# Hybrid S5 and sparse-attention step: chunk scan moved beside the bisection, index scores moved forward

## The reference, cut to what matters

```
h = RMSNorm(x);  [u|q|k|v|q_idx|k_idx|w_idx|g_ssm|g_attn] = h @ W_in
A: state space model: 32 groups x 16 channels, 64 complex states each,
   h_t = a*h_(t-1) + b*u_t (associative scan over positions), y = Re(C h_t) + D u_t,
   y = gelu(y); y = y * sigmoid(y @ w_glu)
B: I[t,s] = sum_h w[t,h] * relu(q_idx[t,h] . k_idx[s]);  top 256 of each causal row;
   softmax attention with QK-RMSNorm and T5 bias over the selected keys
x = x + W_o(sigmoid(g_ssm)*(A @ w_ssm_out) + sigmoid(g_attn)*(B @ w_attn_out))
x = x + W_down relu(W_up RMSNorm(x))^2
```

## Time and profile before

| what | value |
|---|---|
| median of 3 runs | 2018.72 us |
| profiled execution, device time | 2016.42 us |
| its span | 2014.6 us |
| PE busy / DVE busy | 1776.4 (88%) / 998.6 (50%) us |
| ACT busy / POOL busy | 562.2 (28%) / 398.6 (20%) us |
| mean granted PE clock | 0.952 |

### The profile page before, as it was taken

One profiled execution on the slowest core, in us unless ns is written; L12 is line 12 of the kernel. 1 busy time (PEld: TensorE's weight loads), 2 busy tenths in 40 slices (PEclk: granted clock), 3 DMA queues, 4 the chain that ended last, 5 costly groups with the idle time before them and its releaser, 6 DMA issues. The chain is left out here.

```text
span 2014.6 us, 28381 instructions
## 1 busy us (share of the span) xinstructions
PE 1776.4 (88%) x11098; PEld 1572.4 (78%) x11112; DVE 998.6 (50%) x1953; ACT 562.2 (28%) x1069; POOL 398.6 (20%) x213
## 2 busy tenths in 40 slices
PE   2869566999999988885598995999999999999999
PEld 2849335899999955553398995988999999999987
DVE  3845988999995547652143132233333333333334
ACT  4323250222322245441121033222222222222220
POOL 5217100011120000000043134111122111111110
PEclk9979788999999989998699997999999999999999
DMA  5171008353231111006542311111111111111102
GB/s 141 47 119 49 27 16 74 98 161 109 93 99 43 39 50 43 1 1 199 167 152 74 117 56 42 42 42 42 42 42 42 44 56 46 42 42 42 42 21 86
DMA packets 120469, 135.34 MB, mean 67 GB/s; under 512 B 23490, under 2 KB 101282, under 8 KB 120338
## 3 DMA queue, kind: packets, MB, share of 16 engines
q1 hardware_dynamic: 120370, 134.01, 23.5%
HBM read 109.80 MB, written 24.18 MB: 67 GB/s over the span
## 5 line engine op out<-in xcount | busy, mean ns | idle before, releaser
L2510 DVE TENSOR_TENSOR view_at<-psum,view_at 128x512 f32<-128x512 f32 (+1 forms) x288 | 199.3, 692 | 183.0 <-PE psum L141 183.0
L139 PE MATMUL psum<-mix_hi,up_hi 128*128 128x352 f32 x768 | 249.9, 325 | 15.9 <-DVE hid_lo L2501 12.3
L140 PE MATMUL psum<-mix_lo,up_hi 128*128 128x352 f32 x768 | 248.1, 323 | 0.0
L141 PE MATMUL psum<-mix_hi,up_lo 128*128 128x352 f32 x768 | 247.8, 323 | 0.0
L139 PE MATMUL psum<-dn_hi,hid_hi 128*128 128x512 f32 x576 | 227.8, 395 | 0.0
L141 PE MATMUL psum<-dn_hi,hid_lo 128*128 128x512 f32 x576 | 226.8, 394 | 0.0
L140 PE MATMUL psum<-dn_lo,hid_hi 128*128 128x512 f32 x576 | 226.4, 393 | 0.0
L2501 DVE TENSOR_TENSOR hid_lo<-psum,hid_hi 128x352 fp32r<-128x352 f32 x96 | 50.4, 525 | 353.8 <-ACT hid_hi L2467 353.8
L1423 DVE TENSOR_SCALAR_CACHE_REDUCE view_at<-view_at,view_at 128x384 bf16<-128x384 f32 (+6 forms) x231 | 196.0, 912 | 1.2
L139 PE MATMUL psum<-h_hi,w_hi 128*128 128x352 f32 x600 | 195.1, 325 | 0.2 <-issue 0.2
L141 PE MATMUL psum<-h_hi,w_lo 128*128 128x352 f32 x600 | 193.5, 323 | 0.0
(11 more groups left out here) (351 smaller groups left out, 3448.8 us busy)
## 6 DMA issues: line engine op xcount, KB each, us to landing
view_at<-w_in SPq DMA_DIRECT2D x18, 1024.0 KB, 5.4
view_at<-w_up SPq DMA_DIRECT2D x16, 1024.0 KB, 5.6
view_at<-w_down SPq DMA_DIRECT2D x16, 1024.0 KB, 4.9
gate_dram<-view_at SPq DMA_DIRECT2D x48, 176.0 KB, 1.9
view_at<-gate_dram SPq DMA_DIRECT2D x16, 528.0 KB, 4.5
view_at<-cache_k SPq DMA_DIRECT2D x32, 256.0 KB, 3.7
view_at<-cache_v SPq DMA_DIRECT2D x32, 256.0 KB
view_at<-u_dram SPq DMA_DIRECT2D x16, 290.0 KB, 14.9
```

Of the source, the lines that this page charges most:

```text
L139: nc.tensor.matmul(out, lhs[0], rhs[0], start=start, stop=False)
L140: nc.tensor.matmul(out, lhs[0], rhs[1], start=False, stop=False)
L141: return nc.tensor.matmul(out, lhs[1], rhs[0], start=False, stop=stop)
L2510: nc.vector.tensor_tensor(x1[r, i, cols], psum[r, 4 + (2 * par + j) % 4, :], x1[r, i, cols], ALU.add).then_inc(add_done, 1)
```

## The change

In stage 1 the 13 parameter loads other than g1 go from SP's to GpSimd's DMA queue, behind GpSimd's first four instructions; g1 is loaded by SP behind the second x tile and has a semaphore of its own; the first gain waits for it alone. The bias copies get four buffers. The loads of `Uc` leave the stage.

In stage 2 the sets, the start states, `turn` and the scan are gone. The 48 units follow the projections at once, with three pairs of banks instead of four, and 9 value units (chunk 5) stand between them, one after every second pair from unit 5 to unit 37. Page loads go ahead of the load of chunk 5. SP loads `Uc` after the last unit.

In stage 3 PE makes sets and start states, 9 value units, the gates, and only then the output of branch A. ACT copies all sets. POOL builds `turn` and does both rotations of each part; DVE keeps only the real scans, as 8 scans over 128 elements a part, ahead of steps 9, 10, 13 and 16 of the bisection. The loads of the kernel table and of u stand behind the 36th gate. The gelu goes from the gates to behind the 19th q and k unit; state output and bias loads are behind the gates.

```diff
+                sp.dma_start(g1c[:, :], a["norm1_g"].rearrange("l (k p) -> p (l k)", p=P)).then_inc(g1_in, 16)
+            for i in range(2, 4):
+                load_x(i)
...
-                sp.dma_start(bias_dram[h], diag[:, h % 2, :]).then_inc(bias_st[h % 2], 16)
+                sp.dma_start(bias_dram[h], diag[:, h % 4, :]).then_inc(bias_st[h % 4], 16)
...
+            pool.dma_start(par_in[0:GP, 0, :], a["ssm_a_re"].rearrange("l (g h) p -> (l g) (h p)", h=2)).then_inc(par_loaded, 16)
...
+            for r, name in enumerate(("ssm_b_re", "ssm_b_im")):
+                pool.dma_start(Bin[:, r], a[name].rearrange("l (g h) p i -> (l h p) g i", h=2)).then_inc(par_loaded, 16)
+            for r, name in enumerate(("ssm_c_re", "ssm_c_im")):
+                pool.dma_start(cin[:, r], a[name].rearrange("l (m g) o p -> (l g o) m p", g=8)).then_inc(par_loaded, 16)
...
-                    dve.wait_ge(par_loaded, 16 * 14)
+                    dve.wait_ge(g1_in, 16)
                 if i:
                     gain(i - 1)
             gain(NT - 1)
+            dve.wait_ge(par_loaded, 16 * 13)
...
+    FILL = [5 + 4 * n for n in range(NT)]
...
+            for n in range(NT):
+                sp.wait_ge(v_out, n + 1)
+                sp.dma_start(rows(nv, n)[:, 0:WC], vst1[own(n), n % 2, :]).then_inc(v_st[n % 2], 16)
+            load_w(sp, 7)
+            sp.wait_ge(unit_mm, len(UNITS))
+            sp.wait_ge(qiS_done, 2)
+            for t in range(L):
+                sp.dma_start(Uc[GI * t:GI * (t + 1), :, :],
+                             u_dram.rearrange("(g i) t c -> t i g c", i=GI)[L - 1 - t]).then_inc(uc_in, 16)
...
-            act.wait_ge(dve_scanned, 1)
...
-                if u == 12:
+                if u == 20:
                     split_high(act, 6)
+                if u in FILL:
+                    n = FILL.index(u)
+                    act.wait_ge(v_mm, n + 1)
+                    if n >= 2:
+                        act.wait_ge(v_st[n % 2], 16 * (n // 2))
...
-                if u >= 4:
-                    pe.wait_ge(relu_done, u - 2)
+                if u >= 2:
+                    pe.wait_ge(relu_done, u - 1)
...
+                if u + 1 in FILL:
+                    n = FILL.index(u + 1)
+                    if n == 0:
+                        pe.wait_ge(w_lo_done, 6)
+                    if n >= 2:
+                        pe.wait_ge(v_out, n - 1)
+                    for k in range(KD):
+                        last = split_mm(psum[:, 6 + n % 2, 0:WC], h_parts(k, tok0(n), tok0(n) + P), w_parts(5, k, 0, WC),
+                                        k == 0, k == KD - 1)
+                    last.then_inc(v_mm, 1)
...
+    SCAN_AT = {9: 0, 10: 1, 13: 2, 16: 3}
...
+                if n == 35:
+                    sp.wait_ge(m_zero, 1)
+                    for t in range(L):
+                        b = L - 1 - t
+                        sp.dma_start(M[GI * b:GI * (b + 1), :, GI * t:P],
+                                     kern_dram[:, :, 0:P - GI * t]).then_inc(m_in, 16)
+                    for t in range(L):
+                        sp.dma_start(Uy[GI * t:GI * (t + 1), :, :],
+                                     u_dram.rearrange("(g i) t c -> t i g c", i=GI)[L - 1 - t][:, :, 0:YC]).then_inc(uy_in, 16)
...
+            link(pool.memset(S[:, :, :, 0:1], 0.0))
+            pool.wait_ge(out_done, I0 + 1)
...
+            for r, (x, y, op) in enumerate(((start[0], start[1], ALU.subtract), (start[1], start[0], ALU.add))):
+                link(tt(t1, a4[0], x, ALU.mult))
+                link(tt(t2, a4[1], y, ALU.mult))
+                link(tt(t1, t1, t2, op))
+                link(tt(ends[:, r].rearrange("p b g -> p g b"), t1, late[r], ALU.add))
...
+            for k in range(7):
+                if k == 6:
+                    split_low(pool, 7)
...
+            def into_frame(q):
+                sr, si, cr, ci, ta, tb, tc, td = parts(q)
+                link(tt(ta, cr, sr, ALU.mult))
+                link(tt(tb, ci, si, ALU.mult))
+                link(tt(tc, cr, si, ALU.mult))
+                link(tt(td, ci, sr, ALU.mult))
+                link(tt(ta, ta, tb, ALU.add))
+                ins = tt(tc, tc, td, ALU.subtract)
+                link(ins)
+                pool.memset(mark, 0.0).then_inc(rotated, 1)
...
+            def out_of_frame(q):
+                sr, si, cr, ci, ta, tb, tc, td = parts(q)
+                pool.wait_ge(summed, q + 1)
+                link(tt(ta, cr, tb, ALU.mult))
+                link(tt(tc, ci, td, ALU.mult))
+                link(tt(sr, ta, tc, ALU.subtract))
+                link(tt(ta, cr, td, ALU.mult))
+                link(tt(tc, ci, tb, ALU.mult))
+                link(tt(si, ta, tc, ALU.add))
...
+            split_low(pool, 8)
+            into_frame(0)
+            into_frame(1)
+            split_low(pool, 9)
+            out_of_frame(0)
+            into_frame(2)
+            split_low(pool, 10)
+            out_of_frame(1)
+            into_frame(3)
+            split_low(pool, 11)
+            out_of_frame(2)
+            out_of_frame(3)
+            link(pool.tensor_copy(finp, S[:, :, :, NC]))
+            pool.memset(mark, 0.0).then_inc(scanned, 1)
             pool.memset(M, 0.0).then_inc(m_zero, 1)
...
+                if n == 2 * NT:
+                    for mm_ in range(4):
+                        act.wait_ge(yt_in[mm_], 16)
+                        nc.scalar.activation(y2[:, mm_, 0:SEQ].rearrange("p (c t) -> p t c", t=L), Yt[:, mm_, :, 0:NC],
+                                             ACT.Gelu_apprx_tanh).then_inc(gelu_done, 1)
+                        nc.scalar.activation(y2[:, mm_, SEQ:T].rearrange("p (b t) -> p t b", t=NS), Yt[:, mm_, 0:NS, NC + 1:YC],
+                                             ACT.Gelu_apprx_tanh).then_inc(gelu_done, 1)
...
+            def sums(q):
+                dve.wait_ge(rotated, q + 1)
+                ta, tb, tc, td = rot[q % 2]
+                for to, of in ((tb, ta), (td, tc)):
+                    for g in range(4):
+                        along = r8[:, 4 * q + g:4 * q + g + 1].broadcast_to([P, NC])
+                        ins = v.tensor_tensor_scan(to[:, g, :], along, of[:, g, :], 0.0, ALU.mult, ALU.add)
+                ins.then_inc(summed, 1)
             for bit in range(31, -1, -1):
+                if 31 - bit in SCAN_AT:
```

More of the change, by code:

```diff
@@ L698, in hybrid_kernel @@
     HR = H * NS
[L699 to L704, removed]
-    qiT = view(36568, 4, T)
[L706 to L712, removed]
+    qiT = view(36568, 4, T)
+    pg = view(31896, NB, NPG, HD)
+    Rb = view(31896, NG, LS)
+    vst1 = view(33944, 2, WC)
+    kiT = view(34456, T)
+    kw = view(35512, NT, HD + H)
+    kwT = view(50600, T)
+    R = view(50600, 2, SEQ)
+    kbT = view(50600, BG, LS)
     wsc = small(NT, H)
@@ L862, in _ @@
-            t1, t2 = (end_t[:, r] for r in range(2))
-            for r, (x, y, op) in enumerate(((start[0], start[1], ALU.subtract), (start[1], start[0], ALU.add))):
-                link(tt(t1, a4[0], x, ALU.mult))
-                link(tt(t2, a4[1], y, ALU.mult))
-                link(tt(t1, t1, t2, op))
-                link(tt(ends[:, r].rearrange("p b g -> p g b"), t1, late[r], ALU.add))
+            split_low(pool, 4)
             split_low(pool, 5)
-            pool.wait_ge(dve_scanned, 1)
@@ L956, in _ @@
             link(v.memset(wsel, 0.0))
-            dve.wait_ge(turned, 1)
-            for q in range(2):
-                scan(v, link, q)
             dve.wait_ge(kw_ev, 2)
@@ L964, in _ @@
             dve.wait_ge(wsc_done, 1)
-            for q in range(2, 4):
-                scan(v, link, q)
-            v.memset(nmark, 0.0).then_inc(dve_scanned, 1)
             for u, (i, h) in enumerate(UNITS):
@@ L1252, in _, with link @@
         def _(pool):
+            tt = nc.gpsimd.tensor_tensor
+            chain = [0]
+            def link(ins):
+                chain[0] += 1
+                ins.then_inc(pool_chain, 1)
+                pool.wait_ge(pool_chain, chain[0])
+            link(pool.memset(S[:, :, :, 0:1], 0.0))
+            pool.wait_ge(out_done, I0 + 1)
+            start = [S[:, r, :, NC + 1:NC + 1 + NB] for r in range(2)]
+            late = [S[:, r, :, NC + 2 + NB:SC] for r in range(2)]
+            a4 = [aps4[:, r, :].unsqueeze(2).broadcast_to([P, GP, NB]) for r in range(2)]
@@ new lines, in _ @@
+            for k in range(7):
+                if k == 6:
+                    split_low(pool, 7)
+                lo = 1 << k
+                n = lo - 1
+                link(pool.tensor_copy(turn[:, :, :, lo], phase[:, :, k, :]))
+                if not n:
+                    continue
+                er, ei = (phase[:, r, k, :].unsqueeze(2).broadcast_to([P, GP, n]) for r in range(2))
+                fr, fi = (turn[:, r, :, 1:lo] for r in range(2))
+                t1, t2 = (x[:, 0:GP * n].rearrange("p (g c) -> p g c", c=n) for x in turn_t)
+                link(tt(t1, fr, er, ALU.mult))
```

(12 more changed lines are left out.)

362 lines of the change are left out of this document (141 added, 221 removed).

## The result

The changed kernel takes 2034.0 us in the median of 4 runs (2033.0 to 2036.2), the kernel before 2019.3 beside it: ratio 1.0074, 95% interval 1.0057 to 1.0092. It is slower by 15. The forecast's sum was 2034, the value stated 2032, the range 2006 to 2058. The profiled execution has a span of 2031.7 against 2014.6, so 17.1 are to be placed. Among the experiments, the first run of e4 (2617.1 and 2016.0) was profiled in a slow execution, at a clock of 0.64, and its trace is not used.

A forecast was written before the change was run, and what follows sets the result against it. Joins bound stage 1, DVE most of stage 2's score units and the third stretch, PE q and k. Terms -15 - 9 + 32 + 7 = +15 gave 2031, with 2.3 for the median 2034; stated 2032, range 2006 to 2058.

The forecast's parts named there:

- Two of the signs: Signs of a right forecast: stage 2 starting at 134 to 138; PE idle some 50 before its first q and k transposes.
- Front and end of stage 1: Stage 1: 2 won by the earlier first gain, 13 by the earlier end; 15 together.
- The cycle of two pairs and one value unit: Stage 2's score units: P + 2.85 + P + R, P a pair on PE, R one relu; 74 for the stretch.
- 9 + 1 - 1: Stage 2's sum: 9 won, bounds 3 and 18.
- Third stretch: Stretch to the masks, DVE: 14 for scans, 8 for short operations and 10 for scans meeting GpSimd; 32 longer.
- The upper end of 52: Third stretch: upper bound on the 32, if GpSimd wins each race for the ports, 36 where 8 was taken.
- no part in it: Third stretch: PE, with 250 of work and a wait of about 10, is done some 50 before DVE's 314.
- q and k: q and k stretch: the gelu, 11 in ACT's chain, stops PE, 7 lost, bounds 3 and 11; nothing else changes.
- the meetings are no small thing: Against the rival that bisection hardly notices GpSimd: third stretch costs 14 instead of 32, time 2016; chance 0.28.
- GpSimd didn't win every race: Against the rival that GpSimd wins every race in the third stretch: +20 over the forecast, 2054; chance 0.17.
- its DMA queue was quick: Against the rival that GpSimd's queue is slow: the front of stage 1 loses 13 instead of winning 2, 2049; chance 0.12.
- value units did interleave: Against the rival that value units do not interleave in stage 2: 27 more there, 2061; chance 0.04.

The follow-up runs named there:

- e4: The kernel after without DVE's 32 scans, GpSimd's table and rotations as they are: 2012.0 us (0.9972).
- e6: The kernel before with all of the change's stage 1, GpSimd issuing the eight loads of u behind the last bias store: 2015.6 us (0.9990).
- e2: The kernel after with the nine value units of chunk 5 back in the third stretch: 2016.3 us (0.9994).
- e7: The kernel after with value units back in the third stretch, four pairs of banks for the score units, and gelu ahead of q and k: 2000.7 us (0.9920).
- e3: The kernel after without GpSimd's rotation table and its 48 rotations, DVE's scans kept: 2001.3 us (0.9930).
- e1: The kernel after with the loads of branch A's output and the gelu moved ahead of the first q and k unit: 2025.5 us (1.0046).

## Why the prediction was right

The mechanism was right in its main parts, and the sizes nearly. That the sum and the time agree to the microsecond, 2034 and 2034, is luck. For the profiled execution the terms summed to 2031, and it took 2033.5 (its span and the 1.8 around it); the 2.3 that I carried to the median were there 0.5, and the two misses cancel. Each term was within 3, with errors of -3, +2, +1, +1 and +2 in the order of the table. Two of the signs that I had named did not come: stage 2 started at 131.35, not at 134 to 138, and PE was idle 31, not 50.

*Front and end of stage 1.* The front was worth 5.6 (u's projection at 54.0 instead of 59.6), not 2: I had spread the cost of a load on GpSimd's queue over 0 to 2, and it is 0.76. What I had set beside it, a time to the first byte, is not what an issue takes of GpSimd. The end was 12.4 for 13: the store issued 2.0 earlier by the bias copies (I had 3, and the wait for a store stayed), and 10.4 less from issue to barrier. Its mechanism was half right: "no loads stand before it" would have won nothing by itself (e6). I had taken the store's flight from a smaller store (4.5; it is 4.3 to the barrier) without saying that this holds only if no loads fly beside it.

*Stage 2.* The cycle of two pairs and one value unit, P + 2.85 + P + R, gave 74 for 74.1. It is the term that I trust most. Without value units the stretch is 61.6 (e2), and with four pairs of banks as well 54.3 (e7). From the last pair to the barrier it was 23.5, where I had 20 for 22.2 before: the clock was 0.55 in it, against 0.69 before. The microsecond for a projection at the low clock was not there: behind a wait of only 1.94 the clock was 1.00 from 131.35 to 142. The line "9 + 1 - 1" is a slip, since its parts (9.9, -1, -1 and 2) come to 10.

*Third stretch.* +32 forecast, +33.0 measured. The way in which DVE is held was as I had read it; the total is partly luck. From the first to the last count it grew by 40.3. I put each operation that took over 0.08 more than its price alone down to the GpSimd instruction beside it:

| from the first to the last count | forecast | measured |
|---|---|---|
| scans by themselves | 14 | 10.5 |
| scans behind rotations (11 of them, 1.0 each) | 10 | 11.0 |
| one scan behind a split | 0 | 4.4 |
| short operations beside table and rotations | 8 | 17.2 |
| short operations behind splits | in the 8 | -2.6 |

The term that I sized wrong is that of the short operations. In a step beside rotations the first waits half of one, the second goes free and the third waits about 1, as I had said and as the rows at 359 show (0.58, 0.17 and 1.05 where each takes 0.17 alone). That is 1.6 a step, or 19 for the 12 steps, and I cut it to 8 for overlaps with the table and the splits; 17.2 was measured beside GpSimd's short instructions, and the splits took only 2.6 less. What hid this is the masks: they shrank by 7.2, since no split of weights met L1443 and L1450 of the kernel before, which had taken 3.29 and 5.32 there. I had not looked at those two. The upper end of 52 is another slip: its own terms, 14, 36 and 10, come to 60.

*PE in the third stretch.* I said that PE has "no part in it", 50 ahead. It waited 30.8 before its first transposes of q and k, since three waits for weights and stores had taken 28 earlier (7.6, 11.8, 8.9) where I had 10. And DVE's masks wait for PE's last unit of branch A, with 4 to spare. The step was right by a narrow margin, and e3 and e4 crossed it.

*q and k.* 7 forecast for the gelu (by its own terms 11 less 3.2, so 8), 7.8 measured, shown by e1. That "nothing else changes" held by a coincidence. The step from the first transposes to the second takes 5.8 in both kernels: before because a small operation of DVE, beside a split, took 3.82 (at 599.58) and PE waited 2.51 for it, after because PE, behind its idle of 30.8, had a clock of 0.56 from 606 to 612. The 1.7 in the GLU, whose clock is 0.95 against 1.00 before, I had not; it is gone in e2 and e7 and not in e1, and what sets it stays open.

The rivals: the meetings are no small thing (e3: 30), GpSimd didn't win every race (that would be 52 or more where 33 was measured), its DMA queue was quick, and value units did interleave.

What stays open: whether DVE's 15 in scans can be had back by placing them where GpSimd rests. The last eight stood so and took 2.64, but no order with all four parts there was run.

## What to carry to other kernels

Work taken from an engine that sets the time and given to one whose instructions hold it up still costs, but here less than keeping it, since the long instructions beside it were of a kind that isn't held; measure the meetings by taking the other engine's work out. Units moved from a stretch where their engine has time to spare into one that it bounds cost most of their length (18 of 26 here), and putting them back is free. A store that ends a stage is as late as the traffic in flight with it: move the traffic, not the store.

## What the runs showed of the hardware

Loads issued by GpSimd took it 0.48 to 1.33 each, 0.76 in the mean (13), and 0.63 for eight loads of 290 KB; with these eight, issued by 127.4, the block ended at 147.5, behind the last landing at 146.4, though no instruction of that block waited for them. A store of the table landed in 3.8 alone and in 12.4 to 14.5 beside 2.3 MB of loads. Bisection counts (TENSOR_SCALAR_CACHE_REDUCE) were not held by GpSimd (0.61 at 384 elements before and after), while operations of 128x7 and scans of 128 were, up to 4.5 and 4.8. Beside dense rotations of 1.3, one scan of 128 went through for each rotation. After an idle of 6.85 PE ran its next 5.5 at the 1.2 GHz level (granted clock 0.50); in the kernel before the clock was 1.00 through q and k, with idles of 1.59 in it.
